# Key lengths of the RWKV preparation in one row per head, squares and scaled keys on ScalarE, small loads issued a stage earlier

## The chip, the core and the metric

The kernel runs on one core of a Trainium2 chip. The metric is the time of one whole execution on the device in microseconds (us). Each core has TensorE (PE, matrix products), VectorE (DVE), ScalarE (ACT), GpSimd (POOL) and SyncE (SP, which issues most DMAs); they run on their own and meet at semaphores.

## The reference

Two decoder layers run on 512 prompt tokens and 8 requests of 8 tokens, T = 576 token columns in all. Each layer has three mixers side by side (pooling, dilated attention, RWKV-7) and a mixture of 16384 small experts. The change lies in what the RWKV mixer prepares before its recurrence:

```
ps = pf + (p_prev - pf) * mu                              # token shift
w_log = -softplus(-(w0 + tanh(wd) @ w_up)) - 0.5
decay = exp(-exp(w_log))
a = sigmoid(a0 + ad @ a_up)
g = sigmoid(gd) @ g_up
kk = heads(k * k_k)                                       # 6 heads of 64
kk = kk / maximum(sqrt(sum(kk * kk, axis=-1)), 1e-12)     # length 1 per head and token
k = k * (1 + (a - 1) * k_a)
bonus = sum(r * k * r_k, axis=-1) * v                     # per head
```

## The kernel before

All data are kept with channels on the 128 partitions and tokens along a row. The 384 channels of r, k and v are three blocks ("pairs", since a block of 128 channels holds two heads). The program is a chain of stages. A stage is a block in which every engine has its own list of instructions, with semaphores of its own; at its end all engines meet, and SP clears the semaphores. So nothing of a stage starts before the slowest engine of the stage ahead has ended. The order inside a stage is written out by hand.

In each layer `attend_sample` (attention of the 8 requests against their caches) comes right before `rwkv_prepare`. In `attend_sample` SP brings keys and values request by request into two buffers each, and a value load waits until TensorE has used the buffer (L676). TensorE, ScalarE and VectorE then work through the requests one after another.

`rwkv_prepare` works like this:

- SP loads the shift state, the mix factors, the vectors, `rw_wa` (up-projections of decay and `a`) and `rw_g` (up-projection of the gate), L836. VectorE waits for all five.
- VectorE mixes blocks 9 and 10 (low-rank inputs) with the token before (`shift_mix`), then blocks 3 to 5 (k). It makes `kk` = k times a vector (L939) and its squares (L941), then mixes r and v.
- TensorE runs five bursts of six matmuls, 128 output rows by 288 columns each, into six PSUM banks: decay (L848), `a` (L853), gate (L859), sums of squares (L865) and bonus sums (L870). ScalarE reads the banks after each of the first four (L883, L887, L891, L894), and the next burst waits for that, since it writes the same banks. In L865 and L870 the weights are `pair_ones`, a 128x128 matrix with a 64x64 block of ones per head. So the sum over a head's 64 channels comes out 64 times, on all the head's partitions.
- VectorE scales the decay logarithms (L946), scans them (L948), and makes the exponents `prev` and `end` (L951, L955), which ScalarE exponentiates (L896 to L900). It makes the new k (L960, L963) and the bonus product (L968).
- The root of the sums (L894, 128x576 per pair) goes through a maximum (L973) and a reciprocal (L975) on VectorE. GpSimd multiplies `kk` by it (L907), VectorE multiplies `b` by `kk` (L978), and last multiplies the bonus sums with v (L981).

The very first stage of the program (L2439, in `program`) loads the inputs and two constants, and SP waits for them.

Of the kernel before, what the change touches and what calls it, by code (L numbers as in the profile page):

```python
# [37 lines left out]
P = 128  # L38
# [591 lines left out]
def attend_sample(nc, m):  # L630
# [8 lines left out]
    with ExitStack() as ctx:  # L639
# [22 lines left out]
        with stage(nc, "counts_in", "k_in0", "k_in1", "v_in0", "v_in1", "q_in", "scored", "maxed", "expd", "turned",  # L662
                   "turned_in", "valued", "scaled", "back", "back_in", "zeroed", "dve_step") as (block, s):
# [3 lines left out]
            def _(sp):  # L667
# [143 lines left out]
def rwkv_prepare(nc, m, r):  # L811

    rw = m.proj_rw[:]
    halves = [(c, half, slice(half * HALF, (half + 1) * HALF)) for c in range(PAIRS) for half in range(2)]
    with ExitStack() as ctx:
# [7 lines left out]
        mu = ctx.enter_context(sbuf(nc, "rw_mu", [P, NB_RW], F32))
        vec = r.vec
        wa_up = ctx.enter_context(sbuf(nc, "rw_wa", [P, PAIRS * P], F32))
        g_up = ctx.enter_context(sbuf(nc, "rw_g", [P, PAIRS * P], F32))
        ps = ctx.enter_context(psum(nc, "rw_ps", [P, 6, 512], F32))

        with stage(nc, "loaded", "shifted", "stored", "dve_step", "act_step", "gates_in", "w_up", "w_read",
                   "a_up", "a_read", "g_done", "g_read", "squared", "summed", "rooted", "prod", "bonus_sum",  # L830
                   "bonus_read", "decays", "scanned", "lasts", "lengths", "unit", "states_in") as (block, s):
# [13 lines left out]
            def _(pe):  # L845
# [4 lines left out]
                ins.then_inc(s.w_up, 1)  # L850
                pe.wait_ge(s.w_read, 6)
# [22 lines left out]
            def _(act):  # L874
# [5 lines left out]
                nc.scalar.activation(r.g[:, 0, :], diff[:, 10, :], ACT.Sigmoid).then_inc(s.gates_in, 1)  # L880
                act.wait_ge(s.w_up, 1)
# [15 lines left out]
                nc.scalar.activation(r.end[:], r.end[:], ACT.Exp).then_inc(s.decays, 1)  # L897
                nc.scalar.activation(r.prev[:], r.prev[:], ACT.Exp).then_inc(s.decays, 1)
                act.wait_ge(s.decays, 1)
                nc.scalar.activation(r.cum[:], r.cum[:], ACT.Exp).then_inc(s.decays, 1)  # L900

            @block.gpsimd
            def _(pool):
                nc.gpsimd.memset(r.state[:], 0.0)
                for c in range(PAIRS):
                    pool.wait_ge(s.lengths, c + 1)
                    nc.gpsimd.tensor_tensor(r.kk[:, c, :], r.kk[:, c, :], sq[:, c, :], ALU.mult).then_inc(s.unit, 1)  # L907

            @block.vector
            def _(dve):  # L910
# [6 lines left out]
                dve.wait_ge(s.loaded, 80)  # L917
# [18 lines left out]
                st.link(shift_mix(3, 6, lambda n: diff[:, n, :]))  # L936
# [9 lines left out]
                st.link(nc.vector.tensor_scalar(r.ld[:], r.ld[:], -DECAY, None, ALU.mult))  # L946
# [25 lines left out]
                dve.wait_ge(s.rooted, 6)  # L972
                st.link(nc.vector.tensor_scalar(sq[:], sq[:], 1e-12, None, ALU.max))  # L973
# [1675 lines left out]
```

## Time and profile before

| | |
|---|---|
| median of 3 runs | 5326.66 us (5324.56 to 5328.09) |
| the profiled execution, own time | 5332.04 us |
| its span in the trace | 5330.2 us |
| granted TensorE clock, mean | 0.943 |
| TensorE busy | 4778.4 us, 90% of the span |
| VectorE busy | 3141.6 us, 59% |
| ScalarE busy | 1670.6 us, 31% |
| GpSimd busy | 363.3 us, 7% |

The span is the time from the first to the last instruction that the profile shows. Busy shares are means over the whole program; most of TensorE's work is in the experts. `rwkv_prepare` runs twice: from about 331.2 to 389.3 us, and from about 2983.1 to 3041.2 us. A granted clock of 1.0 is 2.4 GHz, of 0.5 is 1.2 GHz. A matmul in float32 appears as two records in the trace, so a burst of six matmuls is "x12".

### The profile page before, as it was taken

To read this page: it belongs to the slowest core of one execution; us is meant where nothing else is said; L and a number is where in the kernel's file an instruction comes from. 1 tells how busy PE (TensorE), PEld (TensorE's weight loads), DVE (VectorE), ACT (ScalarE), POOL (GpSimd) and SP (SyncE) were. 2 spreads that over 40 slices of the span, in tenths; PEclk is the share of its full clock that TensorE was granted. 3 is DMA by queue.
4 is the path that set the end of the run, shared out by engine and by line. 5 is a ranking of instruction groups with operands and counts; after the bars stand their busy time and mean duration, and the time that the engine had idled before them with its cause. 6 is when DMAs were issued, how large, how long until landed. Compare 5 with 4: busy or idle time off the path is not lost. (4 is left out here: it accounts for less than half of the span.)

```text
span 5330.2 us, 99808 instructions
## 1 busy us (share of the span) xinstructions
PE 4778.4 (90%) x39364; PEld 4586.7 (86%) x39364; DVE 3141.6 (59%) x6341; ACT 1670.6 (31%) x2570; POOL 363.3 (7%) x194
## 2 busy tenths in 40 slices
PE   7768596999999999999987676969899999999998
PEld 7647496899999999999985465969899999999998
DVE  3564478875555555557735644888755555555576
ACT  2322222882222222222123222228722222222222
POOL 0200054000000000000002000540000000000000
PEclk9878798999999999999998787989999999999999
DMA  3330121664333333325323301216743333333253
GB/s 96 109 143 1 61 97 47 179 199 179 115 120 133 116 115 116 131 111 177 119 86 125 120 2 70 90 45 192 210 164 130 115 115 117 135 117 115 105 196 120
DMA packets 390832, 631.24 MB, mean 118 GB/s; under 512 B 29184, under 2 KB 327680, under 8 KB 348800
## 3 DMA queue, kind: packets, MB, share of 16 engines
q1 hardware_dynamic: 388640, 620.74, 33.1%
q10 hardware_dynamic: 2016, 8.26, 0.4%
q8 instruction: 98, 1.61, 0.1%
q14 instruction: 78, 0.64, 0.0%
HBM read 526.52 MB, written 152.36 MB: 127 GB/s over the span
## 5 line engine op out<-in xcount | busy, mean ns | idle before, releaser
L228 PE MATMUL ex_op<-ex_ah,ex_vl 128*128 128x288 f32 x3584 | 1066.6, 298 | 7.4 <-DVE ex_acc L2305 6.4
L230 PE MATMUL ex_op<-ex_ah,ex_vh 128*128 128x288 f32 x3584 | 1057.7, 295 | 0.0
L229 PE MATMUL ex_op<-ex_al,ex_vh 128*128 128x288 f32 x3584 | 1056.1, 295 | 0.0
L2305 DVE TENSOR_TENSOR ex_acc<-ex_acc,ex_op 128x576 f32<-128x576 f32 x896 | 672.6, 754 | 549.0 <-PE ex_op L230 535.0
L228 PE MATMUL ex_hp<-x_hi,ex_ul 128*128 128x288 f32 x3072 | 906.2, 295 | 18.4 <-PEq L122 15.8
L230 PE MATMUL ex_hp<-x_hi,ex_uh 128*128 128x288 f32 x3072 | 907.1, 295 | 0.0
L229 PE MATMUL ex_hp<-x_lo,ex_uh 128*128 128x288 f32 x3072 | 906.2, 295 | 0.0
L228 PEld LDWEIGHTS ex_op<-ex_ah,ex_vl 128*128 128x128 f32 x3584 | 674.2, 188 | 14.9 <-DVE ex_acc L2305 14.9
L230 PEld LDWEIGHTS ex_op<-ex_ah,ex_vh 128*128 128x128 f32 x3584 | 673.8, 188 | 0.0
L229 PEld LDWEIGHTS ex_op<-ex_al,ex_vh 128*128 128x128 f32 x3584 | 673.1, 188 | 0.0
L2254 ACT ACTIVATE ex_vh<-ex_v 128x2048 fp32r<-128x2048 f32 x128 | 245.6, 1918 | 1138.1 <-PE ex_op L230 858.7
L228 PEld LDWEIGHTS ex_hp<-x_hi,ex_ul 128*128 128x128 f32 x3072 | 577.9, 188 | 19.2 <-issue 16.2
L229 PEld LDWEIGHTS ex_hp<-x_lo,ex_uh 128*128 128x128 f32 x3072 | 577.8, 188 | 0.0
L230 PEld LDWEIGHTS ex_hp<-x_hi,ex_uh 128*128 128x128 f32 x3072 | 577.8, 188 | 0.0
L2308 DVE TENSOR_TENSOR ex_a<-ex_a,ex_g 128x576 f32<-128x576 f32 x192 | 145.7, 759 | 634.1 <-ACT ex_a L2268 633.6
L2268 ACT ACTIVATE ex_a<-ex_hp 128x576 f32<-128x576 f32 x192 | 125.0, 651 | 798.7 <-PE ex_hp L230 798.7
L2005 PE MATMUL g_ps<-g_a,g_a 128*128 128x128 f32 x2304 | 313.6, 280 | 47.4 <-DVE g_a L1969 26.2
L2005 PEld LDWEIGHTS g_ps<-g_a,g_a 128*128 128x128 f32 x2304 | 289.3, 194 | 58.7 <-DVE g_a L1969 45.6
L2297 DVE TENSOR_TENSOR ex_vl<-ex_v,ex_vh 128x2048 fp32r<-128x2048 f32 x128 | 292.4, 2284 | 0.0
L1969 DVE TENSOR_SCALAR g_a<-iota,i1T,gT 128x128 f32<-128x128 f32 x864 | 245.7, 340 | 0.0
L1964 DVE TENSOR_TENSOR g_a<-iota,i2T 128x512 f32<-128x512 f32 x288 | 198.0, 687 | 77.3 <-PEq L2012 63.0
L2292 DVE TENSOR_TENSOR ex_ul<-ex_u,ex_uh 128x2048 fp32r<-128x2048 f32 x94 | 214.7, 2284 | 19.9 <-ACT ex_uh L2248 19.9
(414 smaller groups left out, 8843.1 us busy)
## 6 DMA issues: line engine op xcount, KB each, us to landing
ex_u<-in_peer_uT SPq DMA_DIRECT2D x128, 1024.0 KB, 7.7
ex_v<-in_peer_v SPq DMA_DIRECT2D x128, 1024.0 KB, 6.8
gate_matrix<-g_stage SPq DMA_DIRECT2D x18, 4096.0 KB, 15.9
ex_g<-gate_matrix SPq DMA_DIRECT2D x128, 576.0 KB, 4.9
dec_k<-in_cache_kT SPq DMA_DIRECT2D x16, 1536.0 KB, 10.4
dec_v<-in_cache_v SPq DMA_DIRECT2D x16, 1536.0 KB, 8.0
out_s_k<-in_cache_k_kept SPq DMA_DIRECT2D x128, 190.5 KB, 6.2
out_s_v<-in_cache_v_kept SPq DMA_DIRECT2D x128, 190.5 KB, 6.2
```

What stands on the lines that cost most here:

```text
L228: nc.tensor.matmul(out, w_lo, x_hi, start=first, stop=False)
L229: nc.tensor.matmul(out, w_hi, x_lo, start=False, stop=False)
L230: return nc.tensor.matmul(out, w_hi, x_hi, start=False, stop=last)
L1964: nc.vector.tensor_tensor(a2[:, b % 4], m.iota[:].unsqueeze(1).to_broadcast([P, TB, P]), i2T[:, bass.ds(w * UNIT + b * TB, TB)].unsqueeze( ...
L1969: ins = nc.vector.tensor_scalar(a1[:, b % 4, n, :], m.iota[:], i1T[:, t], gT[:, t], ALU.is_equal, ALU.mult)
L2005: ins = nc.tensor.matmul(ps[:, q, n, :], a2[:, q, n, :], a1[:, q, n, :], start=True, stop=True)
L2254: nc.scalar.activation(v_hi[:, j], v_raw[:, j], ACT.Copy).then_inc(s.vh, 1)
L2268: nc.scalar.activation(a_raw[:, e, :].rearrange("p (a t) -> p a t", a=2), hp[:, e, :, 0:HALF], ACT.Gelu).then_inc(s.gelud, 1)
L2292: nc.vector.tensor_tensor(u_lo[j][:], u_raw[j][:], u_hi[j][:].bitcast(F32), ALU.subtract).then_inc(s.ul, 1)
L2297: nc.vector.tensor_tensor(v_lo[:, j], v_raw[:, j], v_hi[:, j].bitcast(F32), ALU.subtract).then_inc(s.vl, 1)
L2305: nc.vector.tensor_tensor(a, a, o[:, :, 0:HALF], ALU.add).then_inc(s.added, 1)
L2308: nc.vector.tensor_tensor(a_raw[:, e, :].rearrange("p (u t) -> p u t", u=NU), h.rearrange("p (u t) -> p u t", u=NU), gb[:, j, :, e, :], AL ...
```

## The change

Lines are those of the files; the new kernel's lines are numbered anew. In the sample attention's stage SP issues the five loads of the preparation after the last value load, and waits for them at the end of its list:

```
@@ attend_sample, SP
+                rw = m.rw
+                mixer_loads = ((rw.shift, m.dram.state_shift), (rw.mu, m.dram.rwkv_mu), (rw.vec, m.dram.rwkv_vec),
+                               (rw.wa, m.dram.rwkv_wa), (rw.g, m.dram.rwkv_g))
...
                     values(b)
+                for dst, src in mixer_loads:
+                    sp.dma_start(dst[:], src[m.l]).then_inc(s.mixer_in, 16)
+                sp.wait_ge(s.mixer_in, 16 * len(mixer_loads))
@@ rwkv_prepare
+    quarters = [(slice(q * COLS, (q + 1) * COLS), slice(q * QUARTER, (q + 1) * QUARTER)) for q in range(4)]
...
-                for dst, src in ((shift[:], m.dram.state_shift[m.l]), (mu[:], m.dram.rwkv_mu[m.l]), (vec[:], m.dram.rwkv_vec[m.l]),
-                                 (wa_up[:], m.dram.rwkv_wa[m.l]), (g_up[:], m.dram.rwkv_g[m.l])):
-                    sp.dma_start(dst, src).then_inc(s.loaded, 16)
@@ rwkv_prepare, TensorE
                 ins.then_inc(s.w_up, 1)
+                pe.wait_ge(s.heads_made, 1)
+                pe.wait_ge(s.squared, PAIRS)
+                for rows, t in quarters:
+                    for c in range(PAIRS):
+                        ins = nc.tensor.matmul(ps[rows, 6, 0:QUARTER], heads[:, c, :], sq[:, c, t],
+                                               start=c == 0, stop=c == PAIRS - 1)
+                ins.then_inc(s.summed, 1)
...
                 pe.wait_ge(s.g_read, 6)
-                pe.wait_ge(s.squared, 1)
-                for n, (c, half, t) in enumerate(halves):
-                    ins = nc.tensor.matmul(ps[:, n, 0:HALF], m.pair_ones[:], sq[:, c, t], start=True, stop=True)
-                ins.then_inc(s.summed, 1)
-                pe.wait_ge(s.rooted, 6)
+                pe.wait_ge(s.inverted, 1)
+                for q, (rows, t) in enumerate(quarters):
+                    for c in range(PAIRS):
+                        ins = nc.tensor.matmul(of_quarter(q)[:, c], m.head_back[rows, c, :], length[rows, :],
+                                               start=True, stop=True)
+                ins.then_inc(s.spread, 1)
+                pe.wait_ge(s.unit, 1)
                 pe.wait_ge(s.prod, 1)
@@ rwkv_prepare, ScalarE
+                act.wait_ge(s.k_mixed, 1)
+                for c in range(PAIRS):
+                    nc.scalar.activation(sq[:, c, :], diff[:, 3 + c, :], ACT.Square,
+                                         scale=vec[:, KK, c:c + 1]).then_inc(s.squared, 1)
+                    nc.scalar.activation(r.kk[:, c, :], diff[:, 3 + c, :], ACT.Copy,
+                                         scale=vec[:, KK, c:c + 1]).then_inc(s.scaled, 1)
                 act.wait_ge(s.w_up, 1)
...
+                act.wait_ge(s.summed, 1)
+                nc.scalar.activation(length[:], ps[:, 6, 0:QUARTER], ACT.Sqrt).then_inc(s.rooted, 1)
                 act.wait_ge(s.g_done, 1)
...
-                act.wait_ge(s.summed, 1)
-                for n, (c, half, t) in enumerate(halves):
-                    nc.scalar.activation(sq[:, c, t], ps[:, n, 0:HALF], ACT.Sqrt).then_inc(s.rooted, 1)
                 act.wait_ge(s.scanned, 1)
-                nc.scalar.activation(r.inv[:], r.cum[:], ACT.Exp, scale=-1.0).then_inc(s.decays, 1)
+                nc.scalar.activation(r.inv[:], r.cum[:], ACT.Exp, scale=DECAY).then_inc(s.decays, 1)
@@ rwkv_prepare, GpSimd
+                st.link(nc.gpsimd.memset(heads[:], 0.0))
+                for c in range(PAIRS):
+                    ins = nc.gpsimd.tensor_copy(heads[:, c, 2 * c:2 * c + 2], m.pair_ones[:, 0:P:HD])
+                ins.then_inc(s.heads_made, 1)
...
-                    nc.gpsimd.tensor_tensor(r.kk[:, c, :], r.kk[:, c, :], sq[:, c, :], ALU.mult).then_inc(s.unit, 1)
@@ rwkv_prepare, VectorE
-                dve.wait_ge(s.loaded, 80)
...
-                for c in range(PAIRS):
-                    ins = nc.vector.tensor_scalar(r.kk[:, c, :], k_[:, c, :], vec[:, KK, c:c + 1], None, ALU.mult)
-                st.link(ins)
-                nc.vector.tensor_tensor(sq[:], r.kk[:], r.kk[:], ALU.mult).then_inc(s.squared, 1)
...
-                st.link(nc.vector.tensor_scalar(r.ld[:], r.ld[:], -DECAY, None, ALU.mult))
...
+                dve.wait_ge(s.rooted, 1)
+                st.link(nc.vector.tensor_scalar(length[:], length[:], 1e-12, None, ALU.max))
+                nc.vector.reciprocal(length[:], length[:]).then_inc(s.inverted, 1)
                 dve.wait_ge(s.a_read, 6)
...
-                dve.wait_ge(s.rooted, 6)
-                st.link(nc.vector.tensor_scalar(sq[:], sq[:], 1e-12, None, ALU.max))
-                for c in range(PAIRS):
-                    nc.vector.reciprocal(sq[:, c, :], sq[:, c, :]).then_inc(s.lengths, 1)
-                for c in range(PAIRS):
-                    dve.wait_ge(s.unit, c + 1)
-                    nc.vector.tensor_tensor(r.b[:, c, :], r.b[:, c, :], r.kk[:, c, :], ALU.mult)
+                dve.wait_ge(s.spread, 1)
+                dve.wait_ge(s.scaled, PAIRS)
+                for q, (rows, t) in enumerate(quarters):
+                    ins = nc.vector.tensor_tensor(r.kk[:, :, t], r.kk[:, :, t], of_quarter(q), ALU.mult)
+                ins.then_inc(s.unit, 1)
+                dve.wait_ge(s.unit, 1)
+                nc.vector.tensor_tensor(r.b[:], r.b[:], r.kk[:], ALU.mult)
@@ program, first stage
+            def _(dve):
+                nc.vector.memset(m.head_back[:], 0.0).then_inc(s.zeroed, 1)
...
+                sp.wait_ge(s.zeroed, 1)
+                for q in range(4):
+                    for c in range(PAIRS):
+                        row = 32 * q + 2 * c
+                        sp.dma_start(m.head_back[row:row + 2, c, :], m.dram.c_pair_ones[0:P:HD, :]).then_inc(s.loaded, 16)
+                sp.wait_ge(s.loaded, 16 * (len(loads) + 4 * PAIRS))
```

The lengths now take one row per head: `heads` sends pair c's two heads to rows 2c and 2c+1 of a group of 32 partitions, and each of the four groups holds a quarter of the tokens (144 columns). `head_back` spreads a row over its head's 64 partitions again. The decay's factor moves into the scale of the exponentials. PSUM grows from 6 to 8 banks in this stage.

On TensorE, the stage `rwkv_prepare` before (`rw_ps` is its PSUM, one row a group of matmuls):

```order
L848 MATMUL rw_ps<-rw_wd,rw_wa 128x288 x6
L853 MATMUL rw_ps<-rw_diff,rw_wa 128x288 x6
L859 MATMUL rw_ps<-rwkv_g,rw_g 128x288 x6
L865 MATMUL rw_ps<-rw_sq,pair_ones 128x288 x6
L870 MATMUL rw_ps<-rwkv_bonus,pair_ones 128x288 x6
```

And the same stage now:

```order
L855 MATMUL rw_ps<-rw_wd,rw_wa 128x288 x6
L862 MATMUL rw_ps<-rw_sq,rw_heads 32x144 x12
L867 MATMUL rw_ps<-rw_diff,rw_wa 128x288 x6
L873 MATMUL rw_ps<-rwkv_g,rw_g 128x288 x6
L880 MATMUL rw_ps<-rw_length,head_back 128x144 x12
L886 MATMUL rw_ps<-rwkv_bonus,pair_ones 128x288 x6
```

The sums of squares moved from fourth to second place, and a burst that spreads the inverted lengths is new ahead of the bonus sums.

On ScalarE, the same stage now (`rw_wd`, `rw_diff` are the mixed inputs, `rw_length` the lengths):

```order
L894 ACTIVATE rw_wd<-rw_diff 64x576
L896 ACT_TABLE_LOAD
L896 ACTIVATE rwkv_g<-rw_diff 128x576
L899 ACTIVATE rw_sq<-rw_diff,rw_vec 128x576
L901 ACTIVATE rwkv_kk<-rw_diff,rw_vec 128x576
...
L905 ACTIVATE rwkv_ld<-rw_ps,rw_vec 128x288 x6
L909 ACTIVATE rwkv_b<-rw_ps,rw_vec 128x288 x6
L912 ACT_TABLE_LOAD
L912 ACTIVATE rw_length<-rw_ps 128x144
L915 ACTIVATE rwkv_g<-rw_ps 128x288 x6
L917 ACT_TABLE_LOAD
```

The squares and scaled keys (six instructions, two of which are shown) stand ahead of the reads of the decay burst; the six roots of 288 columns became one of 144, ahead of the gate's reads. There are three table loads, as before.

On VectorE, the end of the stage now (`rwkv_kk` the unit keys, `rwkv_bonus` the bonus):

```order
L965 SCALAR_TENSOR_TENSOR rwkv_cum<-chunk_reset,rwkv_ld 128x576 x3
L968 TENSOR_TENSOR rwkv_prev<-rwkv_cum,rwkv_ld 128x1728
L972 TENSOR_TENSOR rwkv_end<-rwkv_cum 128x512 x3
L972 TENSOR_TENSOR rwkv_end<-rwkv_cum 128x64 x3
L977 TENSOR_SCALAR rw_length<-rw_length 128x144
L978 RECIPROCAL rw_length<-rw_length 128x144
L981 SCALAR_TENSOR_TENSOR rwkv_bonus<-rwkv_b,rw_diff 128x1728
L984 SCALAR_TENSOR_TENSOR rwkv_k<-rwkv_bonus,rw_vec,rw_diff 128x576 x3
L989 SCALAR_TENSOR_TENSOR rwkv_bonus<-rwkv_r,rw_vec,rwkv_k 128x576 x3
L996 TENSOR_TENSOR rwkv_kk<-rwkv_kk,rw_ps 128x3x144 x4
L999 TENSOR_TENSOR rwkv_b<-rwkv_b,rwkv_kk 128x1728
L1002 TENSOR_TENSOR rwkv_bonus<-rw_ps,rwkv_v 128x288 x6
```

The maximum and the reciprocal moved ahead of the new k and shrank to 144 columns; the product with `kk` came over from GpSimd, between the spread and the bonus.

## Rows read from the trace of the kernel before

**Rows 1.** Timeline, start of the preparation: start, length, instruction, [idle before, releaser].

```profile
331.30 0.22 DVE L916 MEMSET rwkv_o<- 128x192 f32 x1 [1.56 <-PEq L122]
...
333.31 0.38 SPq L836 DMA_DIRECT2D rw_g<-in_rwkv_g  x1
...
335.87 1.23 DVE L922 TENSOR_TENSOR rw_diff<-proj_rw 128x1022 f32<-128x1022 f32 x1 [4.35 <-DMA rw_g<-in_rwkv_g]
```

**Rows 2.** Timeline of the preparation in layer 1.

```profile
339.80 6.12 PE L848 MATMUL rw_ps<-rw_wd,rw_wa 64*128 64x288 f32 x12 [10.47 <-ACT rw_wd L878]
341.06 0.68 ACT L880 ACTIVATE rwkv_g<-rw_diff 128x576 f32<-128x576 f32 x1
343.47 1.38 DVE L939 TENSOR_SCALAR rwkv_kk<-rw_diff,rwkv_vec 128x576 f32<-128x576 f32 x3
344.88 1.96 DVE L941 TENSOR_TENSOR rw_sq<-rwkv_kk 128x1728 f32<-128x1728 f32 x1
345.96 2.46 ACT L883 ACTIVATE rwkv_ld<-rw_ps,rwkv_vec 128x288 f32<-128x288 f32 x6 [4.22 <-PE rw_ps L848]
...
348.47 6.13 PE L853 MATMUL rw_ps<-rw_diff,rw_wa 64*128 64x288 f32 x12 [2.55 <-ACT rwkv_ld L883]
...
355.68 1.06 DVE L946 TENSOR_SCALAR rwkv_ld<-rwkv_ld 128x1728 f32<-128x1728 f32 x1
...
357.14 5.74 PE L859 MATMUL rw_ps<-rwkv_g,rw_g 128*128 128x288 f32 x12 [2.55 <-ACT rwkv_b L887]
...
362.83 2.29 DVE L955 TENSOR_TENSOR rwkv_end<-rwkv_cum 128x512 f32<-128x512 f32 x6
362.91 1.93 ACT L891 ACTIVATE rwkv_g<-rw_ps 128x288 f32<-128x288 f32 x6 [5.82 <-PE rw_ps L859]
...
364.89 4.87 PE L865 MATMUL rw_ps<-rw_sq,pair_ones 128*128 128x288 f32 x12 [2.02 <-ACT rwkv_g L891]
...
371.75 1.06 DVE L973 TENSOR_SCALAR rw_sq<-rw_sq 128x1728 f32<-128x1728 f32 x1
...
372.85 10.98 DVE L975 RECIPROCAL rw_sq<-rw_sq 128x576 f32<-128x576 f32 x3
...
386.98 2.28 DVE L981 TENSOR_TENSOR rwkv_bonus<-rw_ps,rwkv_v 128x288 f32<-128x288 f32 x6
```

**Rows 3.** Instructions on `rw_diff`: count, ns least/median/most, first and last start.

```profile
L853 PEld LDWEIGHTS rw_ps<-rw_diff,rw_wa x24: 285/334/334, 348.5 to 3005.2; 64*128 64x128 f32 x24
```

**Rows 4.** Windows: width, busy us of PE, PEld, DVE, ACT, POOL; PEclk, DMA share, GB/s.

```profile
347.00:356.00 9.00, 6.13 (x12) 3.84 (x12) 8.89 (x15) 2.78 (x8) 0.00 (x0) 0.50 0.00 0
...
364.00:372.00 8.00, 5.09 (x13) 3.48 (x14) 7.79 (x13) 4.31 (x11) 0.00 (x0) 0.79 0.00 0
```

**Rows 5.** Timelines of TensorE in the sample attention: small matmuls.

```profile
257.86 3.64 PE L698 MATMUL dec_sps<-dec_k,dec_q 128*32 128x512 f32 x12 [3.91 <-DVE dec_q L767]
```

**Rows 6.** The same, a later stretch.

```profile
281.78 1.99 PE L715 MATMUL dec_tps<-ident,dec_p 96*128 96x48 f32 x16
```

**Rows 7.** Instructions on `dec_v`, from 250 to 335 us.

```profile
L676 SPq DMA_DIRECT2D dec_v<-in_cache_v x6: 332/333/333, 275.5 to 316.4; - x6
...
DMA to landing us min/median/max: 6.3/7.3/8.5
```

**Rows 8.** Timeline, the last request of the sample attention.

```profile
324.45 3.35 PE L730 MATMUL dec_ops<-dec_v,dec_pt 128*32 128x128 f32 x48 [0.51 <-ACT dec_pt L756]
```

**Rows 9.** Timeline, the program's first stage and the start of the second.

```profile
2.53 0.52 SPq L2439 DMA_DIRECT2D iota<-in_c_iota  x1
11.37 1.28 ACT L161 ACT_TABLE_LOAD   x1 [11.37 <-PEq L122]
...
12.60 1.33 SPq L148 DMA_DIRECT2D chunk_masks<-in_c_masks  x2
```

**Rows 10.** The load of `iota`, the last of the first stage.

```profile
DMA to landing us min/median/max: 8.0/8.0/8.0
```

**Rows 11.** Timeline of layer 2: VectorE reads of PSUM with a second operand.

```profile
3046.50 0.56 DVE L1234 TENSOR_TENSOR rp_n<-rp_ps,chunk_masks 128x384 f32<-128x384 f32 x1 [0.27 <-PE rp_ps L1312]
```

More of the change, by code:

```diff
@@ L662, in attend_sample @@
         with stage(nc, "counts_in", "k_in0", "k_in1", "v_in0", "v_in1", "q_in", "scored", "maxed", "expd", "turned",
[L663 removed]
+                   "turned_in", "valued", "scaled", "back", "back_in", "zeroed", "mixer_in", "dve_step") as (block, s):
             k_in, v_in = (s.k_in0, s.k_in1), (s.v_in0, s.v_in1)
@@ L813, in rwkv_prepare @@
     rw = m.proj_rw[:]
+    COLS, QUARTER = 32, T // 4
+    quarters = [(slice(q * COLS, (q + 1) * COLS), slice(q * QUARTER, (q + 1) * QUARTER)) for q in range(4)]
     halves = [(c, half, slice(half * HALF, (half + 1) * HALF)) for c in range(PAIRS) for half in range(2)]
@@ L819, in rwkv_prepare, with of_quarter @@
         tmp = r.bonus
-        shift = ctx.enter_context(sbuf(nc, "rw_shift", [P, NB_RW, REQ], F32))
+        heads = ctx.enter_context(sbuf(nc, "rw_heads", [P, PAIRS, COLS], F32))
+        length = ctx.enter_context(sbuf(nc, "rw_length", [P, QUARTER], F32))
         last_p = ctx.enter_context(sbuf(nc, "rw_last_p", [P, NB_RW, 1], F32))
         last_s = ctx.enter_context(sbuf(nc, "rw_last_s", [P, NB_RW, REQ], F32))
[L823 to L831, printed above, removed]
+        shift, mu, vec, wa_up, g_up = m.rw.shift, m.rw.mu, r.vec, m.rw.wa, m.rw.g
+        ps = ctx.enter_context(psum(nc, "rw_ps", [P, 8, 512], F32))
+        def of_quarter(q):
+            return ps[:, q, 0:PAIRS * QUARTER].rearrange("p (c t) -> p c t", c=PAIRS)
+        with stage(nc, "shifted", "k_mixed", "heads_made", "stored", "dve_step", "pool_step", "gates_in", "w_up", "w_read",
+                   "a_up", "a_read", "g_done", "g_read", "squared", "scaled", "summed", "rooted", "prod", "bonus_sum",
+                   "bonus_read", "decays", "scanned", "lasts", "inverted", "spread", "unit", "states_in") as (block, s):
             @block.sync
             def _(sp):
-                for dst, src in ((shift[:], m.dram.state_shift[m.l]), (mu[:], m.dram.rwkv_mu[m.l]), (vec[:], m.dram.rwkv_vec[m.l]),
-                                 (wa_up[:], m.dram.rwkv_wa[m.l]), (g_up[:], m.dram.rwkv_g[m.l])):
-                    sp.dma_start(dst, src).then_inc(s.loaded, 16)
                 sp.dma_start(r.states[:], m.dram.state_wkv[m.l]).then_inc(s.states_in, 16)
@@ L891, in _ @@
                     nc.scalar.activation(r.g[:, c, t], ps[:, n, 0:HALF], ACT.Copy).then_inc(s.g_read, 1)
-                act.wait_ge(s.summed, 1)
-                for n, (c, half, t) in enumerate(halves):
-                    nc.scalar.activation(sq[:, c, t], ps[:, n, 0:HALF], ACT.Sqrt).then_inc(s.rooted, 1)
                 act.wait_ge(s.scanned, 1)
-                nc.scalar.activation(r.inv[:], r.cum[:], ACT.Exp, scale=-1.0).then_inc(s.decays, 1)
-                nc.scalar.activation(r.end[:], r.end[:], ACT.Exp).then_inc(s.decays, 1)
-                nc.scalar.activation(r.prev[:], r.prev[:], ACT.Exp).then_inc(s.decays, 1)
+                nc.scalar.activation(r.inv[:], r.cum[:], ACT.Exp, scale=DECAY).then_inc(s.decays, 1)
+                nc.scalar.activation(r.end[:], r.end[:], ACT.Exp, scale=-DECAY).then_inc(s.decays, 1)
+                nc.scalar.activation(r.prev[:], r.prev[:], ACT.Exp, scale=-DECAY).then_inc(s.decays, 1)
                 act.wait_ge(s.decays, 1)
-                nc.scalar.activation(r.cum[:], r.cum[:], ACT.Exp).then_inc(s.decays, 1)
+                nc.scalar.activation(r.cum[:], r.cum[:], ACT.Exp, scale=-DECAY).then_inc(s.decays, 1)
             @block.gpsimd
             def _(pool):
+                st = Steps(pool, s.pool_step)
+                st.link(nc.gpsimd.memset(heads[:], 0.0))
+                for c in range(PAIRS):
+                    ins = nc.gpsimd.tensor_copy(heads[:, c, 2 * c:2 * c + 2], m.pair_ones[:, 0:P:HD])
+                ins.then_inc(s.heads_made, 1)
                 nc.gpsimd.memset(r.state[:], 0.0)
-                for c in range(PAIRS):
-                    pool.wait_ge(s.lengths, c + 1)
-                    nc.gpsimd.tensor_tensor(r.kk[:, c, :], r.kk[:, c, :], sq[:, c, :], ALU.mult).then_inc(s.unit, 1)
             @block.vector
@@ L1506, in rwkv @@
         r.o = sb("rwkv_o", [P, NT, HEADS * HD])
-        r.vec = sb("rwkv_vec", [P, 7, PAIRS])
+        r.vec = m.rw.vec
         rwkv_prepare(nc, m, r)
@@ L2431, in program @@
         m.ident, m.iota = sb("ident", [P, P]), sb("iota", [P, P])
+        m.head_back = sb("head_back", [P, PAIRS, P])
         m.g1, m.g2 = sb("g1", [P, KD]), sb("g2", [P, KD])
-        with stage(nc, "loaded") as (block, s):
+        with stage(nc, "loaded", "zeroed") as (block, s):
+            @block.vector
+            def _(dve):
+                nc.vector.memset(m.head_back[:], 0.0).then_inc(s.zeroed, 1)
             @block.sync
@@ L2439, in _ @@
                     sp.dma_start(dst, src).then_inc(s.loaded, 16)
-                sp.wait_ge(s.loaded, 16 * len(loads))
+                sp.wait_ge(s.zeroed, 1)
[4 more added lines that the diff above has]
+                sp.wait_ge(s.loaded, 16 * (len(loads) + 4 * PAIRS))
         with nc.Fori(0, LAYERS) as l:
@@ L2454, in program @@
                     m.proj_rw = pb.enter_context(sbuf(nc, "proj_rw", [P, NB_RW, T], F32))
+                    m.rw = Parts()
+                    m.rw.shift, m.rw.mu, m.rw.vec, m.rw.wa, m.rw.g = (
+                        pb.enter_context(sbuf(nc, "rw_" + name, shape, F32))
+                        for name, shape in (("shift", [P, NB_RW, REQ]), ("mu", [P, NB_RW]), ("vec", [P, 7, PAIRS]),
+                                            ("wa", [P, PAIRS * P]), ("g", [P, PAIRS * P])))
                     with ExitStack() as pa:
```

4 lines of the change are left out of this document (2 added, 2 removed).

## The prediction

> **What bounds the kernel now.** I read the page for where the engines are busy, then the timeline of both preparations, the windows for the clock, and the tiles that the moved work touches. The page's long groups are the experts' matmuls, which the change leaves alone. So the question is the length of one stage, which runs twice: nothing of the next stage starts before it ends, and each microsecond off its end is one off the kernel. The reader should see three things. First, the stage stands still at its start: VectorE waits 4.35 us for the last load [rows 1]. Second, from there VectorE works nearly without a gap to the end at 389.26 (386.98 + 2.28), and TensorE waits for it or for ScalarE [rows 2]. Third, the tail is VectorE's alone: from 371.75 on it does the maximum, three reciprocals in 10.98 us, the product with `b` and the bonus [rows 2]. TensorE's last burst (like L865, 4.87 us) ended long before. The second layer's stage has the same rows in the same order, within 0.2 us; the sum is made for layer 1 and doubled.
>
> **The change part by part.** I walk the new stage through with durations of before, since two chains now run side by side, and where they meet decides.
>
> Start. VectorE has nothing to wait for after its memset (331.30 + 0.22, next instruction about 331.50) instead of 335.87: 4.37 us earlier [rows 1]. The five loads now follow the value load issued at 316.4, which lands within 6.3 to 8.5 us [rows 7]. SP issues them by about 319.4; even if they land only after 8.5 us more, that is 327.9, while the next stage's first instruction on VectorE comes at 331.30 [rows 1]. (I take the loads in the order of their queue.) They stand behind the value load, and TensorE takes those values at 324.45 [rows 8], 8.05 us after its issue, released by ScalarE. I cost them at nothing; that work hides them. If they slowed the value load by its full spread (8.5 - 7.3 = 1.2 us), the price would be about 1.2 us a layer.
>
> VectorE. All it does before L939 is 4.37 earlier, so the mixed k are done at 343.45 - 4.37 = 339.07. L939 and L941 are gone (from 343.47 to about 346.76 before the next started, with 1.38 + 1.96 busy: 3.3 us), and so is L946 (1.06) [rows 2]. The mixes of r and v end at 355.66 - 4.37 - 3.3 = 347.95; the scans, `prev` and `end`, which took from L946's end, 356.74, to 362.83 + 2.29 = 365.12, so 8.35, end at 356.3 [rows 2].
>
> TensorE and ScalarE. The decay burst starts 4.37 earlier, 335.43 to 341.55, at 6.12 us [rows 2]. ScalarE meets the mixed k at 339.1 and does six instructions of 576 columns at 0.68 each alone [rows 2]; following each other I take 0.62. The third square (fifth of six) ends at 342.2, the sixth instruction at 342.8. Its reads of the decay burst (2.46) end at 345.3, before VectorE needs them (347.95). So the squares cost ScalarE 3.7 us, and VectorE's mixing covers them.
>
> The sums of squares are 24 records of 144 columns. There is no such burst before. From above: 12 records of 288 columns took 6.13 with a granted clock of 0.50 (1.2 GHz), and 24 of 144 move as many columns. L865, in part at the higher clock (mean 0.79 in its window), took 4.87 [rows 2, 4]. From below: L698 has 12 records of 512 columns on 32 output rows, three column groups in turn, in 3.64 us, 0.30 a record [rows 5]. At the rate of 6.13/12/288 = 1.77 ns a column that would be 0.91 one by one, so three groups run side by side. Here the order is by group, three matmuls into the same rows before the next group, so only neighbours at a change of group can overlap. The range is 1.5 (four groups wholly side by side, 6.13/4) to 6.1; I take 5.8, near the serial row. It runs 342.25 to 348.05.
>
> A turn from one tile shape to another is not priced by a row of its own; I add 0.2. The `a` burst runs 348.25 to 354.4, ScalarE reads it until 356.85 (+2.46). Then a table load of 1.28 [rows 9], and one root of 144 columns at about 0.3 (L891 has 1.93 for six of 288, 0.32 each when they follow one another): 358.4.
>
> Here the chains meet: VectorE came at 356.3 and waits to 358.4, 2.1 us. Maximum of 144 columns (1.06/1728 of L973 a column, plus start-up): 0.15. Reciprocal: 10.98/1728 x 144 = 0.92. With links 359.6. The new k and the bonus product took what lies between 365.12 and L973's start at 371.75, 6.6 us [rows 2], now until 366.2.
>
> TensorE meanwhile: gate burst from 356.9, 5.74 [rows 2], to 362.7; ScalarE reads it for 1.93 until 364.7. Then the spread: 24 records of 144 columns, weights of 32 rows by 128 columns. Bounds: 1.5 (four row groups side by side) and 6.1; L715, 16 records of 48 columns with 128-column weights in 1.99 us, 0.124 each [rows 6], says that such small records need at least 24 x 0.124 = 3.0 in this order. It stands where L865 stood, after the same pause, so I take between 4.87 and 6.1: 5.3, until 370.1. VectorE waits 366.2 to 370.1 and multiplies `kk` from PSUM: four of 432 columns, 0.56 for 384 [rows 11], 0.52 apart: 2.15, until 372.3. The bonus burst waits for that, since it overwrites the banks, and takes 4.87 to 6.1, say 5.4: 377.75. VectorE's product with `b` (2.0) lies beside it. Last the bonus, 2.28: 380.1. ScalarE's table load and four exponentials (1.28 + 6.3 after 364.7) end at 372.4, hidden.
>
> So the stage ends at 380.1 instead of 389.26: 9.15 us. There are three more semaphores to clear here and one in the stage ahead; no row prices one, I take 0.15 (range 0 to 0.4). Net 9.0 a layer, 18.0 in all. Note where the rest went: VectorE loses 4.4 + 3.3 + 1.1 + 9.9 of reciprocals, and more at the product with `b`, in all about 19 us; it then waits about 2.1, 3.9 and 3.5 us for the TensorE and ScalarE chain.
>
> **A rule weighed.** L853's twelve weight loads are recorded at 0.334 us each [rows 3], and yet its twelve matmuls came in 6.13 us, 0.51 each at 1.2 GHz, of which 288 columns twice are 0.48. So the loads lay under the matmuls although all use the same 64 rows. The Trainium skill (TensorE: Matmul & The Clock Gate, Part 3: Packing small matmuls) says that a weight load overlaps running matmuls only where its row group is another. By the rule both new bursts would pay for their loads; by this row they do not. It is rival B below.
>
> First stage. SP issues 12 more loads of 1 KB from 3.05 us on, at 0.52 (`iota`) to 0.66 (1.33 for two) each [rows 9]: the last at 8.8 to 10.3. Before, the stage's last landing was that of `iota`, 2.53 + 8.0 = 10.5 [rows 9, 10], behind the bulk of the inputs. A load of this kind that stands behind nothing was issued at 333.31 and used at 335.87, 2.56 later [rows 1]; so the twelfth lands between 10.5 and 12.9, and the stage ends 0 to 2.4 us later. I take 0.6. VectorE's memset there is done long before.
>
> Sum: 18.0 - 0.6 = 17.4 us. From the profiled execution's own 5332.04 (span 5330.2 and 1.8 around it) that is 5314.6. That execution lies 5.4 above the median of the runs, so the time that I predict is 5326.66 - 17.4 = 5309.3.
>
> **The rivals.**
> A. The four groups of 32 really run side by side. Then the sums take 1.5 to 3, the `a` burst starts at ScalarE's 345.3, and the spread takes 3. The meeting at the root is then VectorE's (356.3, root already there), the bonus product ends at 364.1, the gate burst at 359.6, reads at 361.5, spread 364.5, `kk` 366.7, bonus burst 372.1, end 374.5: 14.7 a layer, 5298. For it: L698's three groups. Against: there the group changes with each matmul, here it does not. A granted clock of 1.0 for most of the bursts would bring a part of the same: up to 4 us a layer, 5301.
>
> B. Weight loads lie open: 24 loads of 128 columns at 0.334 add 8.0 in the spread, and 24 of 32 columns in the sums something from 0 to 8.0, taken as 4.0. That is 12.0 a layer against 9.0 gained: 3.0 lost, twice, and 0.6: 5333.3, slower than before. It decides from 9.0/48 = 0.19 us a record on. Against: L853 above, and L715 with 0.124 for the whole record.
>
> C. The early loads and the first stage cost more than they seem (value load late by 1.2, first stage 2.4 later), and all new bursts run at 1.2 GHz (0.3 + 0.8 + 0.7): 9.0 - 3.0 = 6.0 a layer, 12.0 - 2.4 = 9.6: 5317.
>
> D. The change does its work but the end is not moved: VectorE was not the bound. Against: no gap in its rows from 335.87 on. No chance to speak of.
>
> **How the numbers follow.** Main case 0.76, from 5304 to 5314 (clock in the bursts about 2 a layer either way, first stage 1.7). A 0.12 with its clock part, B 0.04, C 0.08. The range reaches into A and C: 5301 to 5317. A change under 0.2% (10.7 us) can hardly be told from none here; faster by more means below 5316.0: main and A and a little of C, 0.90; within 0.2%: 0.07; slower, which needs more than B's mean price: 0.03.
>
> **What would show it.** In the new profile: VectorE's first mix starts 0.2 us after its memset, in both layers. The squares lie between the k mix and the reads of the decay burst. VectorE idles about 2 us for the root, 4 for the spread, 3.5 for the bonus sums. The sums burst takes 5 to 6 us and delays the `a` burst; the stage is about 49 us from the memset to the last bonus product instead of 58. The prediction is wrong if a burst of 24 records takes under 3 or over 7 us, if ScalarE loads a table between its squares and its sigmoids, or if a stage outside this one moves by more than 2 us.

## The result

The changed kernel took 5292.96 us (median of 4 runs, 5289.0 to 5296.65); the kernel before, beside it, 5327.38 us. The ratio is 0.9932 with a 95% interval of 0.9916 to 0.9948: 34.4 us less. The prediction was 17.4 us less, 5309.3, with a range down to 5301. The direction was right and the size half of what came.

The profile of after has a span of 5287.2 us (that execution took 5289.0, the least of the four), a mean granted clock of 0.947 and VectorE busy 3113.1 us. The timeline of the changed kernel's preparation in layer 1 (start, length, engine, line, operation; in brackets the idle time before it and what ended it) answers to [rows 1, 2]:

```profile
328.77 0.22 DVE L939 MEMSET rwkv_o<- 128x192 f32 x1 [1.61 <-PEq L122]
...
328.91 1.16 DVE L944 TENSOR_TENSOR rw_diff<-proj_rw 128x1022 f32<-128x1022 f32 x1
...
332.77 6.13 PE L855 MATMUL rw_ps<-rw_wd,rw_wa 64*128 64x288 f32 x12 [6.02 <-ACT rw_wd L894]
...
340.02 3.08 PE L862 MATMUL rw_ps<-rw_sq,rw_heads 128*32 128x144 f32 x24 [1.13 <-ACT rw_sq L899]
340.45 2.42 ACT L905 ACTIVATE rwkv_ld<-rw_ps,rw_vec 128x288 f32<-128x288 f32 x6
...
343.03 6.13 PE L867 MATMUL rw_ps<-rw_diff,rw_wa 64*128 64x288 f32 x12
...
351.70 4.90 PE L873 MATMUL rw_ps<-rwkv_g,rw_g 128*128 128x288 f32 x12 [2.55 <-ACT rwkv_b L909]
352.96 0.29 ACT L912 ACTIVATE rw_length<-rw_ps 128x144 f32<-128x144 f32 x1
353.51 0.23 DVE L977 TENSOR_SCALAR rw_length<-rw_length 128x144 f32<-128x144 f32 x1
353.77 1.05 DVE L978 RECIPROCAL rw_length<-rw_length 128x144 f32<-128x144 f32 x1
...
358.62 3.74 PE L880 MATMUL rw_ps<-rw_length,head_back 32*128 32x144 f32 x24 [2.01 <-ACT rwkv_g L915]
...
362.40 2.15 DVE L996 TENSOR_TENSOR rwkv_kk<-rwkv_kk,rw_ps 128x432 f32<-128x432 f32 x4 [1.13 <-PE rw_ps L880]
...
364.60 5.27 PE L886 MATMUL rw_ps<-rwkv_bonus,pair_ones 128*128 128x288 f32 x12 [2.24 <-DVE rwkv_kk L996]
369.91 2.28 DVE L1002 TENSOR_TENSOR rwkv_bonus<-rw_ps,rwkv_v 128x288 f32<-128x288 f32 x6 [3.37 <-PE rw_ps L886]
```

The reader should see that the steps stand in the predicted order, but that the burst of sums (L862) took 3.08 us, not 5.8, and the spread (L880) 3.74, not 5.3. VectorE does not wait for the root at all, and waits 1.13 us for the spread instead of 3.9. From the memset to the last product it is 43.4 us; it was 58.0, and the walk gave 48.8.

In layer 2 the `a` burst runs at the higher clock. The timeline there:

```profile
2970.37 3.04 PE L862 MATMUL rw_ps<-rw_sq,rw_heads 128*32 128x144 f32 x24 [1.13 <-ACT rw_sq L899]
...
2973.34 3.17 PE L867 MATMUL rw_ps<-rw_diff,rw_wa 64*128 64x288 f32 x12
...
2980.32 0.29 ACT L912 ACTIVATE rw_length<-rw_ps 128x144 f32<-128x144 f32 x1
...
2983.86 0.23 DVE L977 TENSOR_SCALAR rw_length<-rw_length 128x144 f32<-128x144 f32 x1
...
2985.94 2.96 PE L880 MATMUL rw_ps<-rw_length,head_back 32*128 32x144 f32 x24 [2.02 <-ACT rwkv_g L915]
...
2991.65 2.15 DVE L996 TENSOR_TENSOR rwkv_kk<-rwkv_kk,rw_ps 128x432 f32<-128x432 f32 x4
```

`a` took 3.17 us instead of 6.13. The root lay ready 3.2 us before VectorE came for it, the spread ended at 2988.9, and VectorE waited for nothing until the bonus sums.

The table cuts the spans by stage. "Preparation" is from its first ScalarE instruction to that of the next stage. "First stage" ends where ScalarE begins to compute in the second stage (its table load of 1.28 us is counted in). "Outside" is all the rest.

| kernel | first stage | preparations | outside | span |
|---|---|---|---|---|
| before | 12.7 | 60.1, 60.1 | 5197.3 | 5330.2 |
| before, second profile | 12.5 | 60.2, 60.2 | 5198.9 | 5331.7 |
| after | 14.0 | 45.7, 44.1 | 5183.3 | 5287.2 |
| after, second profile | 13.9 | 46.2, 44.0 | 5193.3 | 5297.4 |

So the preparations gave 30.4 us, the first stage took 1.4 back, and the rest, 14.0 us in this pair of profiles and 5.4 of the medians' 34.4, lies outside the change.

### The profile page after: what moved, and what is told of

The parts are those of the page before. It is cut to its first block and busy times, and to the rows that moved or that the text cites. A ratio compares the mean times of both kernels' runs of the same rounds, so it can differ in the third digit from the quotient of the medians.

```text
span 5287.2 us, 99980 instructions
## 1 busy us (share of the span) xinstructions
PE 4772.3 (90%) x39436; PEld 4585.6 (87%) x39436; DVE 3113.1 (59%) x6332; ACT 1674.6 (32%) x2572; POOL 357.5 (7%) x196
```

## The experiments

**The same kernels again**, to see what "outside" is worth.

> The kernel before, profiled once more, to see how much the stages outside the preparation differ from one execution to the next. Theory 1 (the 13.7 us that the first pair of profiles shows outside the two preparations are for the most part the spread between executions, through the granted clock): the stages outside the preparation together come out several us shorter than the 5209.7 us of the first profile of before, while the two preparations stay at 60.1 us each. Rival (the change itself makes the other stages faster): the other stages repeat within 2 us, each stage within 0.5 us.

> The changed kernel, profiled once more. Theory 1: the two preparations repeat within 1 us (45.7 and 44.1), the stages outside, 5197.4 us in the first profile, come out some 3 to 8 us longer. Rival: they repeat within 2 us, and every stage that was shorter than before is shorter again by the same amount.

Measured: 5333.5 and 5299.2 us. The preparations repeated within 0.5 us. Outside, before repeated within 1.6 us, which is what the rival said and not theory 1. After came out 10.0 longer than in its first profile, more than the 3 to 8 of theory 1. So the first profile of after was on the short side. That a kernel with the old lengths varies as much, this pair does not show (the placement kernel below does).

**The bursts by themselves.** Added behind the bonus sums (shortened here, with comments that are not in the file; the spread likewise, behind the bonus products):

```
+                for rows, t in quarters:                # as it is (L891)
+                    for c in range(PAIRS):
+                        nc.tensor.matmul(ps[rows, 6, 0:QUARTER], heads[:, c, :], sq[:, c, t], ...)
+                for c in range(PAIRS):                  # group changes each time (L895)
+                    for rows, t in quarters:
...
+                for rows, t in quarters:                # one group, ps[0:COLS, ...] (L899)
```

> The changed kernel with bursts added behind the bonus sums whose results nobody reads: the sums burst as it is, then with the partition group changing at each matmul, then all 12 into one partition group; behind the bonus products the spread burst as it is, with the row group changing at each matmul, and all from one row group. Theory (partial overlap: the matmuls of one group follow one another, those of the next group run beside them in part): at 1.2 GHz the one-group sums take 5.8 us (24 records of 0.24), the burst as it is 3.1, the one with turns 1.5 to 2; the same order for the spread: 5.8, 3.7 at a mixed clock, 1.5 to 3. At 2.4 GHz half of each. Rival (a 32-row or 32-column matmul is just shorter than I took it, with no overlap between groups): all three versions of a burst take the same time at the same clock.

Three answers of this kernel's trace, one for each version of the sums (count, then min, median and max ns of a record, first and last start in us):

```profile
L891 PE MATMUL rw_ps<-rw_sq,rw_heads x24: 286/286/310, 371.5 to 373.0; 128*32 128x144 f32 x24
...
L895 PE MATMUL rw_ps<-rw_sq,rw_heads x24: 286/286/310, 372.6 to 373.7; 128*32 128x144 f32 x24
...
L899 PE MATMUL rw_ps<-rw_sq,rw_heads x24: 286/286/286, 373.4 to 376.2; 128*32 128x144 f32 x24
```

The granted clock was 1.00 throughout. First to last start: 1.5 us as it is, 1.1 with turns (between the tails of its neighbours), 2.8 in one group. The spreads gave 1.8, 1.1 and 2.9. A single record lasts 286 ns in each. So the rival falls: in one group a narrow matmul took 0.12 us a record at 2.4 GHz, and the gain is overlap between groups, also in the order as it is. The one-group spread reloads its weights in the same 32 rows for each record and still took 0.13 us a record, so the weight loads were hidden there too.

**Turns in the kernel itself.**

```
-                for rows, t in quarters:
-                    for c in range(PAIRS):
+                for c in range(PAIRS):
+                    for rows, t in quarters:
```

(and the same in the spread)

> The changed kernel with the loops over pairs and quarters exchanged in the sums and in the spread, so that the partition group changes with each matmul. Theory (overlap between groups): the sums burst falls from 3.1 to 1.5 to 2 us, but ScalarE's reads of the decay burst (until 342.9) then hold the second burst, so that only about 0.1 us comes of it; the spread falls from 3.7 to 1.5 to 2.5 us and its 1.1 us of waiting on VectorE goes: the stage is 1.0 to 1.5 us shorter, the kernel 2 to 3 us (ratio to before 0.9928). Rival (no overlap): both bursts and the stage as they were, ratio 0.9932.

The timeline of TensorE alone in this kernel, the same stage of layer 1:

```profile
341.95 1.67 PE L862 MATMUL rw_ps<-rw_sq,rw_heads 128*32 128x144 f32 x24 [1.13 <-ACT rw_sq L899]
344.86 6.12 PE L867 MATMUL rw_ps<-rw_diff,rw_wa 64*128 64x288 f32 x12 [1.24 <-ACT rwkv_ld L905]
353.53 5.33 PE L873 MATMUL rw_ps<-rwkv_g,rw_g 128*128 128x288 f32 x12 [2.55 <-ACT rwkv_b L909]
360.88 1.43 PE L880 MATMUL rw_ps<-rw_length,head_back 32*128 32x144 f32 x24 [2.01 <-ACT rwkv_g L915]
365.43 6.13 PE L886 MATMUL rw_ps<-rwkv_bonus,pair_ones 128*128 128x288 f32 x12 [3.11 <-DVE rwkv_kk L996]
```

The bursts shrank as expected (3.08 to 1.67, 3.74 to 1.43). The kernel did not: 5291.8 us, ratio 0.9932 (0.9919 to 0.9946). That interval is too wide to tell 2 to 3 us, but the stages tell: preparations of 45.5 and 45.4, in layer 1 only 0.2 to 0.7 shorter than in the two profiles of after, in layer 2 1.3 to 1.4 longer. The first gain ended in a wait (1.24 before `a`, for the decay reads), and the bonus burst took 6.13 instead of 5.27: all of it at 1.2 GHz. In layer 2 `a` ran at 1.2 GHz too (6.12 instead of 3.17), and the bonus burst took 6.10 instead of 4.79. My 2 to 3 us were a miss.

**Both bursts doubled**, to give them about the lengths that the prediction had.

```
-                for rows, t in quarters:
+                for rows, t in [x for x in quarters for _ in range(2)]:
```

(and the same in the spread)

> The changed kernel with each quarter of the sums and of the spread multiplied twice (same results), so that these two bursts take about what the prediction gave them: 6.2 instead of 3.1 us (predicted 5.8) and about 6.5 instead of 3.7 (predicted 5.3). Theory (the two bursts' lengths are the step that failed in the stage, the rest of the walk stands): the preparation, 46 and 44 us from its first ScalarE instruction to the next stage's, grows to 51 to 53 us, as the walk gave with its lengths (48.8 + 2.3 = 51.1), and VectorE waits for the root and for the spread as the walk said. Rival (the bursts lie beside VectorE's work and something else made the stage short): 46 to 48 us.

Preparations of 51.3 and 50.2 us. Timeline and windows (width, busy us of the engines, then the granted clock) in layer 1:

```profile
339.52 6.21 PE L862 MATMUL rw_ps<-rw_sq,rw_heads 128*32 128x144 f32 x48 [1.13 <-ACT rw_sq L899]
345.66 3.17 PE L867 MATMUL rw_ps<-rw_diff,rw_wa 64*128 64x288 f32 x12
...
359.04 8.79 PE L880 MATMUL rw_ps<-rw_length,head_back 32*128 32x144 f32 x48 [2.01 <-ACT rwkv_g L915]
```

```profile
339.50:345.60 6.10, 6.08 (x48) 4.91 (x48) 6.03 (x10) 2.86 (x7) 0.00 (x0) 0.73 0.00 0
345.60:348.80 3.20, 3.20 (x14) 2.17 (x12) 3.13 (x3) 0.00 (x0) 0.00 (x0) 1.00 0.00 0
```

Lengthening the two bursts lengthened the stage by 5 to 6 us, so they lie on its path, and the rival falls. That the sum meets the walk's 51.1 is in part luck, for the parts came out otherwise. The sums took 6.21 us only because the clock rose within the burst (0.73 is the mean of its window). The spread, nearly all at 1.2 GHz, took 8.79, not 6.5: with twelve records a group, too, only the last three of each ran beside the next group. The sums were followed by `a` at 2.4 GHz (3.17), so the wait for the root did not come, and VectorE waited 7.11 us for the spread alone.

**The parts by themselves.** The early loads added to the kernel before:

```
+                for dst, src in mixer_loads:
+                    sp.dma_start(dst[:], src[m.l]).then_inc(s.mixer_in, 16)
+                sp.wait_ge(s.mixer_in, 16 * len(mixer_loads))
```

> The kernel before with the one edit that the five small loads are issued in the sample attention. Theory: each preparation (from its first ScalarE instruction to that of the next stage, 60.1 us before) is 4.4 us shorter, 55.7, since VectorE has no gap at its start and the rest is VectorE's chain as before; the sample attention is no longer than before (73.4 to 75.1). 8.8 us in all, ratio 0.9983. Rival (the loads delay the last value load): 1.2 us a layer come back in the sample attention, 6.4 us in all.

5318.1 against 5326.8 us, ratio 0.9982 (0.9973 to 0.9991), as expected; preparations 55.3 and 55.3, 4.8 less each. The sample attention took 74.6 and 73.7, as before. The term stands (4.37 predicted).

The lengths as before, in the changed kernel:

```
-                for rows, t in quarters:
...
+                for n, (c, half, t) in enumerate(halves):
+                    ins = nc.tensor.matmul(ps[:, n, 0:HALF], m.pair_ones[:], sq[:, c, t], start=True, stop=True)
+                ins.then_inc(s.summed, 1)
```

> The changed kernel with the lengths made as before (sums on all partitions as the fourth burst, 288-column roots, maximum and reciprocals of 576 columns, product with kk on GpSimd); loads, squares on ScalarE and the decay factor as changed. Theory (VectorE's chain without a gap): each preparation 60.1 - 4.4 - 3.3 - 1.1 = 51.3 us, so that the lengths are worth 51.3 - 45 = 6 us of the 15 a layer. Rival (the chain of TensorE and ScalarE would by now set the end here too): 53 us or more.

Preparations of 56.8 and 57.1 us: the rival, not the theory, and the most telling miss. From its timeline:

```profile
347.82 6.13 PE L860 MATMUL rw_ps<-rw_diff,rw_wa 64*128 64x288 f32 x12 [4.03 <-ACT rwkv_ld L896]
...
362.70 2.28 DVE L977 SCALAR_TENSOR_TENSOR rwkv_bonus<-rwkv_r,rw_vec,rwkv_k 128x576 f32<-128x576 f32 x3
363.75 1.28 ACT L907 ACT_TABLE_LOAD   x1
363.78 4.87 PE L872 MATMUL rw_ps<-rw_sq,pair_ones 128*128 128x288 f32 x12 [2.02 <-ACT rwkv_g L904]
368.69 1.93 ACT L907 ACTIVATE rw_sq<-rw_ps 128x288 f32<-128x288 f32 x6 [3.66 <-PE rw_ps L872]
370.63 1.28 ACT L909 ACT_TABLE_LOAD   x1
370.64 1.06 DVE L982 TENSOR_SCALAR rw_sq<-rw_sq 128x1728 f32<-128x1728 f32 x1 [5.67 <-ACT rw_sq L907]
```

VectorE waits 5.67 us for the roots. In the kernel before it came to them with no wait, but only just. Its bonus product ended at 371.61 and the last root at 371.73, so the other chain was as long:

```profile
369.33 2.28 DVE L968 SCALAR_TENSOR_TENSOR rwkv_bonus<-rwkv_r,rwkv_vec,rwkv_k 128x576 f32<-128x576 f32 x3
369.80 1.93 ACT L894 ACTIVATE rw_sq<-rw_ps 128x288 f32<-128x288 f32 x6 [3.66 <-PE rw_ps L865]
```

With the old lengths the squares and the decay factor buy nothing. The squares even cost: they hold up ScalarE's reads of the decay burst, so TensorE waits 4.03 us ahead of `a` instead of 2.55, and the preparations are 1.5 and 1.8 us longer than with the early loads alone (55.3). The new lengths are worth 11.1 and 13.0 us a layer, since they shorten both chains. In the changed kernel the sums burst lies in that wait.

Squares and scaled keys back on VectorE, in the changed kernel:

```
+                for c in range(PAIRS):
+                    ins = nc.vector.tensor_scalar(r.kk[:, c, :], k_[:, c, :], vec[:, KK, c:c + 1], None, ALU.mult)
+                st.link(ins)
+                nc.vector.tensor_tensor(sq[:], r.kk[:], r.kk[:], ALU.mult).then_inc(s.squared, 1)
```

> The changed kernel with scaled keys and squares made by VectorE again. Theory (after the lengths shrank VectorE's chain and the chain of TensorE and ScalarE are nearly even, VectorE waits only 1.1 us for the spread and 3.4 us for the bonus sums): the 3.4 us on VectorE show with 2.2 to 2.3 us in each preparation, 48.0 and 46.4. Rival (TensorE and ScalarE set the end, as predicted): less than 0.5 us a preparation, since in my walk VectorE waited 2.1 + 3.9 us ahead of the unit keys.

48.9 and 48.9: 2.7 to 3.2 more than after in layer 1, 4.7 to 4.9 in layer 2. So the rival falls. The size was 0.9 off in layer 1 and 2.5 in layer 2: in after, VectorE had no wait ahead of the unit keys in layer 2 that could take up a part of the 3.4 us, and the bonus burst took 6.13 us here in both layers (5.27 and 4.79 in after).

**Placement alone.** The kernel before with the tiles where the changed kernel has them:

```
+        m.head_back = sb("head_back", [P, PAIRS, P])
```

(and the five tiles of the preparation allocated early; the "outside" of this expectation includes the first stage)

> The kernel before, with the tiles of the preparation (shift, mu, vec, wa, g) and the unused tile of the spreading weights placed in SBUF where the changed kernel has them, and nothing else. The first two profiles of before have 5210.0 and 5211.3 us outside the preparations, the four of kernels with the new placement 5197 to 5207. Theory 1 (part of the gain outside comes from where the later stages' tiles lie): outside the preparations 5200 to 5207 us, the two preparations at 60.1 each, ratio 0.9980 to 0.9990. Rival (placement does nothing; the clock's state that the shorter preparation leaves behind, or chance): outside 5208 to 5213, ratio 1.0000 within its interval.

5328.0 against 5326.8 us, ratio 1.0001 (0.9992 to 1.0010), which leaves out the 0.9980 to 0.9990 of theory 1: placement does nothing that shows. Its profiled execution was the shortest of its eleven, with a span of only 5316.9, preparations of 59.9 and 60.2, and 5184.3 outside. So a kernel with the old preparation too has executions that are 13 us shorter outside.

**A better version.** First the bonus sums split alone:

```
-                pe.wait_ge(s.unit, 1)
                 pe.wait_ge(s.prod, 1)
                 for n, (c, half, t) in enumerate(halves):
-                    ins = nc.tensor.matmul(ps[:, n, 0:HALF], ...)
+                    if n == 4:
+                        ins.then_inc(s.bonus_sum, 1)
+                        pe.wait_ge(s.unit, 1)
+                    ins = nc.tensor.matmul(ps[:, (n + 4) % 8, 0:HALF], ...)
```

> The changed kernel with the bonus sums in banks 4 to 7 and then 0 and 1: the first four need no longer wait until the unit keys are read out of banks 0 to 3, only the last two. Theory (that wait is on the path): the burst starts with the spread's end, at the bonus product or at latest then, about 2 us earlier, and four of the six last products on VectorE overlap it: VectorE waits under 1 us instead of 3.4 at the end, the preparation is 2.5 to 3.5 us shorter, 42 to 43 us. Rival (VectorE is the bound by then): under 1 us.

41.2 and 41.8, 5288.5 us in its one run: 4.6 less than after in layer 1 and 2.3 in layer 2, around the 2.5 to 3.5 expected. The clock is in both numbers. In layer 1 the spread ran at a granted clock of 1.00 and took 2.06 us instead of 3.74; in layer 2 the bonus burst ran at 1.2 GHz, 6.13 instead of 4.79. Then with the turns, and with the twelve loads in each layer's normalisation stage:

```
+                            loads += [(m.head_back[32 * q + 2 * c:32 * q + 2 * c + 2, c, :], m.dram.c_pair_ones[0:P:HD, :])
+                                      for q in range(4) for c in range(PAIRS)]
```

> The changed kernel with three edits: the loops of the sums and of the spread exchanged, so that the partition group changes with each matmul; the bonus sums split as in the run before; and the twelve loads of the spreading weights moved from the first stage to the loads of each layer's normalisation stage, which lie beside its work. Theory: the preparation 41 to 42.5 us, the first stage back from 14.0 to 12.7 us; 9 us below the changed kernel, 5284, ratio to before 0.9918. Rival (the granted clock takes back what shorter bursts give, as in the run with turns alone): 45 us a preparation, 5291, 0.9932.

From the timeline of this kernel, the tail of layer 1's preparation (L888 is the bonus burst, L998 VectorE's scaling by the spread lengths, L1006 the last product):

```profile
363.36 2.15 DVE L998 TENSOR_TENSOR rwkv_kk<-rwkv_kk,rw_ps 128x432 f32<-128x432 f32 x4
363.38 6.03 PE L888 MATMUL rw_ps<-rwkv_bonus,pair_ones 128*128 128x288 f32 x12 [0.92 <-DVE rwkv_bonus L991]
...
365.54 1.96 DVE L1001 TENSOR_TENSOR rwkv_b<-rwkv_b,rwkv_kk 128x1728 f32<-128x1728 f32 x1
...
367.63 1.55 DVE L1006 TENSOR_TENSOR rwkv_bonus<-rw_ps,rwkv_v 128x288 f32<-128x288 f32 x4
369.45 0.82 DVE L1006 TENSOR_TENSOR rwkv_bonus<-rw_ps,rwkv_v 128x288 f32<-128x288 f32 x2 [0.27 <-PE rw_ps L888]
```

5285.5 us (5281.2 to 5286.8; 5284 was expected), against 5324.4 for before, ratio 0.9923 (0.9909 to 0.9937). Preparations 41.8 and 41.5, first stage 12.8. VectorE now waits 0.27 us in the tail. The stages show the gain over the changed kernel plainly; the two ratios' intervals overlap. The turns add nothing to the split.

## Why the prediction was wrong

Step by step, in layer 1, from VectorE's memset on:

- Start: right (no gap; VectorE's mixes begin 0.14 after the memset's start).
- Squares on ScalarE: 0.67 us each, not 0.62; right in effect.
- **The sums burst, 5.8 us: this term failed.** It took 3.08, at a granted clock of 0.50. The prediction said that only neighbours at a change of group can overlap, and took nearly nothing off for it. The starts of the 24 records in the trace, 0.24 us apart within a group, show how much it is: each next group began right behind the third record of the group ahead, with three of its six still to come. The four groups so began at 0, 0.46, 0.94 and 1.43 us. With 1.20 us for the last group's records and 0.45 for its last one to end that is the 3.08, and for a part of it three groups ran at once. I stood near the serial row and gave the partial case no estimate of its own.
- `a` burst and its reads: as long as predicted in layer 1, 2.7 earlier. In layer 2 and in the doubled kernel it took 3.17 at 2.4 GHz: a gain that the prediction had only as a bound, beside rival A.
- Gate burst: 4.90, not 5.74, for its later part at the higher clock.
- **The spread, 5.3 us: the same error**; 3.74 and 2.96.
- Wait for the root, 2.1: it fell away. Wait for the spread: 1.13 and none, not 3.9. Bonus burst 5.27 against 5.4, its wait 3.37 against 3.5: right.
- First stage: 1.4 against 0.6, inside its bounds of 0 to 2.4.
- The weighed rule: the weight loads stayed hidden, and rival B did not come. The one-group bursts took 0.12 (sums) and 0.13 us (spread) a record at 2.4 GHz, where 144 columns twice are 0.12: the loads added at most 0.01, and B needed 0.19.

In the walk the errors of layer 1 add up: 2.7 (sums) + 0.8 (gate) + 1.6 (spread) + 0.3 of small ones = 5.4 us, which is 48.8 - 43.4. Layer 2 is another 1.6 to 2.1 shorter: `a` at 2.4 GHz takes away VectorE's wait for the spread, and the bonus burst is shorter by 0.5. Rival A was the mechanism, by half, and its own price (14.7 a layer) came close to the measured 14.4 and 16.0. In layer 2 that is luck, since A had not put in the clock. That A was given 0.12 was the misjudgement.

One thing more went wrong: 5.4 us of the medians' difference lie outside the preparations, where I had put nothing. Without them the time would be 5298.4, still below the range of 5301 to 5317, so the stage alone is enough to make the range fail. What is shown of the 5.4: placement is not the cause, and "outside" differs by 10 us between two executions of the changed kernel and by 14.6 between executions of kernels with the old lengths. 5.4 is also within the ratio's interval (8.5 us either way). And yet it is not all chance. The thirteen profiled executions can be cut by stage. The stage that projects the mixers' outputs (`mix_out`) took 70.1 to 70.5 us, on average 70.3, in the five with the old lengths, and 68.3 to 70.0, on average 68.6, in the eight with the new ones; its granted clock was 0.88 with the old and mostly 0.90 with the new. The routing stage (`route`) took 265.0 on average against 263.9. Together this is 2.8 us a layer, 5.5 in all. The kernel with the lengths as before, which has all the other edits, stays with the old ones. So the difference comes with the lengths; by which way they reach stages that begin some 170 us later no run tells, and that cause stays open.

## What to carry to other kernels

When a change shortens two chains that were nearly even, walk both with several values for each uncertain burst: here the end moved by what was shortened in both, and an edit on one of them alone bought little. Give partial overlap a case of its own: bursts on different partition groups in group order took about half of the serial time, with turns little more than a quarter. And look for the next wait that is made by a buffer and not by data: spreading the bonus sums over free banks was worth more (3.4 us a layer on average, 45.7 and 44.1 to 41.2 and 41.8) than making the burst ahead of it shorter. Read such a gain in more than one stage, since the clock mixed into each of them here.

## What the runs showed of the hardware

Float32 matmuls on different 32-row or 32-column groups overlapped without being interleaved in the program: 24 records of 144 columns took 3.08 us at 1.2 GHz in group order, 1.67 with turns, and about 5.9 would be serial by estimate (0.12 a record in one group at 2.4 GHz, 0.24 at 1.2). In group order the next group started right behind the record after which three more of the group ahead were to come: the third with six records a group, the ninth with twelve. So longer groups overlapped less: 48 records took 8.79 us.

The granted clock of a burst was not the same in every stage that ran the same code. Behind sums in group order the `a` burst ran at 1.2 GHz (6.13 us) in five of ten stages and at 2.4 GHz or nearly (3.17 to 3.35) in the other five. The first preparations of after and of the kernel with the added bursts are the same up to there, with sums of 3.08 and 3.05 us; `a` took 6.13 in one and 3.17 in the other. Behind the sums with turns (1.67) it ran at 1.2 GHz in all four stages, behind the doubled sums at 2.4 GHz in both. The bonus burst took 5.8 to 6.1 us in the four stages with spreads of 1.0 to 1.5 us, and 4.7 to 5.6 in after's two profiles with spreads of 3.0 to 3.7. But it took 6.13 also behind spreads of 3.45 (squares back on VectorE) and 2.71 (bonus sums split). So a shorter burst often went with a slower next one, and then its gain was lost; that the shortening is the cause is not shown.
